# Per-row expert weights: fetched from a table in DRAM instead of spread by products

## What is computed

```python
scores = jax.nn.sigmoid((t @ p['w_router']).astype(jnp.float32))
...
_, e_idx = lax.top_k(jnp.where(e_mask, biased, -jnp.inf), TOP_K)       # TOP_K = 6 of 64
w = jnp.take_along_axis(scores, e_idx, axis=-1)
w = w / jnp.sum(w, axis=-1, keepdims=True) * ROUTE_SCALE
combine = jnp.einsum('tk,tke->te', w, jax.nn.one_hot(e_idx, N_EXPERTS, dtype=jnp.float32)).astype(h.dtype)
gte = jnp.einsum('td,edf->tef', t, p['w_gate_e'])
upe = jnp.einsum('td,edf->tef', t, p['w_up_e'])
routed = jnp.einsum('tef,efd->td', jax.nn.silu(gte) * upe * combine[:, :, None], p['w_down_e'])
```

## Time and profile before

| | |
|---|---|
| median of 3 runs | 992.41 us (990.46 to 992.43) |
| the profiled execution | 994.2 us |
| its span, first to last instruction | 992.6 us |
| mean granted TensorE clock | 0.978 |
| TensorE busy | 923.7 us (93%), weight loads beside it 568.5 (57%) |
| VectorE / ScalarE / GpSimd busy | 339.0 (34%) / 198.4 (20%) / 120.1 (12%) |
| DMA over the span | 324.37 MB, mean 327 GB/s, 57799 packets |

### The profile page before, as it was taken

How to read it: one execution, slowest core, us unless ns; L and a number is a source line. 1 busy time by engine, 2 the same in 40 slices (tenths; PEclk the granted TensorE clock), 3 DMA queues, 4 the chain that set the end, 5 groups by cost and what they waited for, 6 DMA issues and landing times.

```text
span 992.6 us, 18757 instructions
## 1 busy us (share of the span) xinstructions
PE 923.7 (93%) x7759; PEld 568.5 (57%) x7759; DVE 339.0 (34%) x850; ACT 198.4 (20%) x492; POOL 120.1 (12%) x150
## 2 busy tenths in 40 slices
PE   4799999997999689589899999999999999999997
PEld 3688888875565467435755445444444544544542
DVE  0433760046344688616332322221122122222214
ACT  2000110325222277015111111111011111111112
POOL 0000000041573000000110110111011011111100
PEclk9999999999999799889999999999999999999999
DMA  9785666453797736796799999999999999999961
GB/s 374 306 316 237 241 275 234 190 158 134 247 357 261 300 124 236 272 423 268 283 361 413 421 424 421 420 424 422 395 409 425 422 419 422 422 421 423 420 285 67
DMA packets 57799, 324.37 MB, mean 327 GB/s; under 512 B 15089, under 2 KB 25186, under 8 KB 36530
## 3 DMA queue, kind: packets, MB, share of 16 engines
q1 hardware_dynamic: 44930, 304.50, 76.2%
q0 software_dynamic: 11056, 18.47, 5.4%
q10 hardware_dynamic: 1728, 0.18, 0.1%
HBM read 325.59 MB, written 15.74 MB: 344 GB/s over the span
## 4 chain that ended last, share of the span: by engine, by line
PE 49%; DVE 1%; ACT 0%; issue 0%
PE bank L2215 24%; PE bank L2140 12%; PE bank L2151 7%; PE bank L2124 4%; PE bank L2255 1%; PE bank L2161 1%; PE bank L2203 1%; DVE slot_b L2545 0%; DVE slot_b L2553 0%; ACT xt L2337 0%; PE bank L2180 0%; PE bank L2188 0%; ACT slot_b L2363 0%; DVE inv L2552 0%; DVE hh L2444 0%
## 5 line engine op out<-in xcount | busy, mean ns | idle before, releaser
L367 PE MATMUL bank<-h,ring 128*128 128x264 f32 x672 | 154.6, 391 | 2.4 <-DVE h L243 1.8
L367 PEld LDWEIGHTS bank<-h,ring 128*128 128x128 f32 x672 | 127.8, 192 | 26.6 <-issue 3.0
L2346 ACT ACTIVATE sge<-bank 64x256 f32<-64x256 f32 x64 | 24.1, 377 | 409.4 <-PE bank L2215 409.4
L2444 DVE TENSOR_TENSOR hh<-sge,bank 64x256 f32<-64x256 f32 x64 | 27.1, 423 | 227.3 <-ACT sge L2346 227.3
L2215 PE MATMUL bank<-done_out,xt 128*64 128x256 f32 x832 | 95.6, 382 | 0.0
L2215 PE MATMUL bank<-ring,xt 128*64 128x256 f32 x800 | 94.9, 391 | 0.8 <-ACT xt L2337 0.8
L2140 PE MATMUL bank<-ring,ht 128*32 128x512 f32 x336 | 80.2, 598 | 0.0
L2389 DVE COPY sq<-bank 128x512 f32<-128x512 f32 x64 | 44.3, 692 | 102.8 <-PE bank L2140 102.8
L1554 POOL DMA_INDIRECT xg<-tok_rows,tab_g x32 | 32.1, 1002 | 361.4 <-PE bank L2124 349.7
L2215 PEld LDWEIGHTS bank<-done_out,xt 128*64 128x64 f32 x832 | 58.6, 139 | 27.1
L2215 PEld LDWEIGHTS bank<-ring,xt 128*64 128x64 f32 x800 | 57.8, 142 | 28.5 <-issue 3.3
(11 more groups left out here) (476 smaller groups left out, 1197.7 us busy)
## 6 DMA issues: line engine op xcount, KB each, us to landing
ring<-in_w_units SPq DMA_DIRECT2D x28, 2048.0 KB, 10.6
done_out<-in_w_e SPq DMA_DIRECT2D x26, 2048.0 KB, 19.9
ring<-in_w_e SPq DMA_DIRECT2D x25, 2048.0 KB, 19.8
slot_b<-in_w_e SPq DMA_DIRECT2D x13, 2048.0 KB, 20.7
ring<-in_w_e SPq DMA_DIRECT2D x21, 1024.0 KB, 20.9
slot_b<-in_w_e SPq DMA_DIRECT2D x11, 1024.0 KB, 23.2
done_out<-in_w_e SPq DMA_DIRECT2D x11, 1024.0 KB, 19.3
row_of<-in_w_e SPq DMA_DIRECT2D x11, 1024.0 KB, 22.3
```

What stands on the lines that cost most here:

```text
L367: mm = pe.matmul(bank[:, t % NB, 0:T], w[:, j, k, :], h[:, k, :], start=(k == 0), stop=(k == KD - 1))
L2346: act.activation(sg[e % 2][:, :], bank[0:LB, 4, 0:FE], ACT.Silu).then_inc(sg_ready, 1)
L2444: dve.tensor_tensor(hh[e % 2][:, :], sg[e % 2][:, :], bank[LB:2 * LB, 4, 0:FE], ALU.mult).then_inc(hh_ready, 1)
```

## The change

The products that spread the weights are gone. VectorE works out, at the start of the stage, a table of places `tab_w` (row number times 64, plus the expert), in SBUF that another list has left; SP writes `wgt` to a DRAM table `weight_tab` of 264 x 64 numbers in three stores, once `wgt` is ready; and GpSimd issues for each pair one more indirect transfer, which fetches for each of the 128 slots one number of 4 bytes into a column of `wv`. `weight_matrix` takes its weights from that column. The fetch for pair 0 waits for the table. The product for the last samples is replaced by the same column, behind the loop.

```diff
@@ SP, in the loop over experts
                             if e + SLOTS < NE:
                                 load_gu(sp, e + SLOTS)
+                            if e == 0:
+                                sp.wait_ge(wgt_ready, 1)
+                                for a, n, lo in ((0, P, 0), (2, P, P), (1, TS, TP)):
+                                    sp.dma_start(weight_tab[lo * NE:(lo + n) * NE, :].rearrange("(t e) o -> t (e o)", e=NE),
+                                                 wgt[0:n, a, :]).then_inc(tab_stored, 16)
@@ GpSimd
+                        def gather_weights(q):
+                            if q == 0:
+                                pool.wait_ge(tab_stored, 48)
+                            if q >= 2:
+                                pool.wait_ge(w_ready, q - 1)
+                            pool.indirect_dma_start(wv[:, q:q + 1], None, weight_tab,
+                                                    bass.IndirectOffsetOnAxis(ap=tab_w[:, q:q + 1].bitcast(U32), axis=0),
+                                                    bounds_check=T * NE - 1, oob_is_err=False).then_inc(wv_in[q % 2], 16)
                         for q in range(NPAIR):
                             if q + AHEAD < NPAIR:
                                 gather(pool, q + AHEAD)
+                            gather_weights(q)
                             if q >= 2:
                                 scatter_samples(q - 2)
@@ TensorE
-                        def weight_rows(q):
-                            if q == 0:
-                                pe.wait_ge(wgt_ready, 1)
-                            for l in range(2):
-                                for e in (2 * q, 2 * q + 1):
-                                    lo = l * LB + e % 2 * HB
-                                    mm = pe.matmul(bank[lo:lo + HB, 7, P:2 * P], wgt[:, 2 * l, e:e + 1].to_broadcast([P, HB]), ident,
-                                                   start=True, stop=True)
-                            mm.then_inc(wrow_done, 1)
...
-                            if e >= 2:
-                                pe.wait_ge(w_ready, e // 2)
...
-                            if e == LAST_AT:
-                                last_weights()
-                            elif e == LAST_AT + 1:
-                                pe.wait_ge(last_ready, 1)
-                            if e % 2:
-                                weight_rows(e // 2)
@@ VectorE, weights()
+                            place_f = wmat[0][:, 0:NPAIR]
+                            dve.memset(wv, 0.0)
+                            link(dve.tensor_scalar(place_f, tok_f[:, :], float(NE), ccol("second"), ALU.mult, ALU.add))
+                            link(dve.scalar_tensor_tensor(tab_w[:, :], ccol("count")[:, 0:NPAIR], 2.0, place_f, ALU.mult, ALU.add))
@@ VectorE, weight_matrix(q)
-                            dve.wait_ge(wrow_done, q + 1)
+                            dve.wait_ge(wv_in[q % 2], 16 * (q // 2 + 1))
...
-                            dve.scalar_tensor_tensor(wmat[q % 2][:, :], iota, tok_f[:, q:q + 1], bank[:, 7, P:2 * P],
-                                                     ALU.is_equal, ALU.mult).then_inc(w_ready, 1)
+                            dve.tensor_scalar(wmat[q % 2][:, :], iota, tok_f[:, q:q + 1], wv[:, q:q + 1],
+                                              ALU.is_equal, ALU.mult).then_inc(w_ready, 1)
@@ VectorE, in the loop and behind it
-                            elif e == LAST_AT:
-                                dve.wait_ge(last_done, 1)
-                                dve.scalar_tensor_tensor(w_last[:, 0:TS], samples, tok_f[0:LB, NPAIR - 1:NPAIR], bank[0:LB, 7, 256:256 + TS],
-                                                         ALU.is_equal, ALU.mult).then_inc(last_ready, 1)
...
+                        dve.tensor_scalar(w_last[:, 0:TS], samples, tok_f[0:LB, NPAIR - 1:NPAIR], wv[0:LB, NPAIR - 1:NPAIR],
+                                          ALU.is_equal, ALU.mult).then_inc(last_ready, 1)
```

More of the change, by code:

```diff
@@ L112 @@
                   ("valid", NT), ("later", NBLK - NE),
-                  ("count", MAXOVER), ("same_head", NH), ("code", NT), ("side", 4), ("pair", NE // 2)):
+                  ("count", MAXOVER), ("same_head", NH), ("code", NT), ("side", 4), ("pair", NE // 2), ("second", 1)):
     CONSTS[_name] = (_at, _at + _n)
@@ L122 @@
 SHARED_S_AT = 40
-LAST_AT = 50
 def build(nc, io):
@@ L1504, in build @@
         tok_rows = nc.dram_tensor("tok_rows", [T, D], F32, kind="Internal").ap()
+        weight_tab = nc.dram_tensor("weight_tab", [T * NE, 1], F32, kind="Internal").ap()
         choice_rows = nc.dram_tensor("choice_rows", [T * TOPK, D], F32, kind="Internal").ap()
@@ L1994, in build @@
                 tok2 = slot_b[:, 5 * (NBLK - NE):6 * (NBLK - NE)]
+                tab_w, wv = tok_i, tok_j[:, :].bitcast(F32)
                 more_f = slot_b[:, 6 * (NBLK - NE):6 * (NBLK - NE) + (ROUNDS - 1) * HB].rearrange("p (r b) -> p r b", b=HB)
@@ L2008, in build @@
                 ht_done, ht_ready, y_ready = sem("ht_done", ph), sem("ht_ready", ph), sem("y_ready", ph)
-                comb_done, wgt_ready, wrow_done, w_ready = (sem("comb_done", ph), sem("wgt_ready", ph), sem("wrow_done", ph),
-                                                            sem("w_ready", ph))
+                comb_done, wgt_ready, w_ready = sem("comb_done", ph), sem("wgt_ready", ph), sem("w_ready", ph)
+                wv_in = [sem(f"wv_in{i}", ph) for i in range(2)]
                 cnt_done, over_ready, w6_ready, spread_done, wc_ready = (sem("cnt_done", ph), sem("over_ready", ph), sem("w6_ready", ph),
@@ L2023, in build @@
                 scattered, read_back = sem("scattered", ph), sem("read_back", ph)
-                shs_done, shs_took, last_done, last_ready = sem("shs_done", ph), sem("shs_took", ph), sem("last_done", ph), sem("last_ready", ph)
+                shs_done, shs_took, tab_stored, last_ready = sem("shs_done", ph), sem("shs_took", ph), sem("tab_stored", ph), sem("last_ready", ph)
                 half_scaled, rest_ready = sem("half_scaled", ph), sem("rest_ready", ph)
@@ L2190, in shared_rows @@
                             mm.then_inc(shs_done, 1)
[L2192 to L2197, removed]
                         def shared_down(n):
@@ L2666, in constants @@
     put("side", 2 * (r[:, None] // NE) + r[:, None] % 2 == np.arange(4)[None, :])
+    put("second", r[:, None] // HB % 2 - 2)
     put("pair", r[:, None] % NE // 2 == np.arange(NE // 2)[None, :])
```

## The result

The changed kernel takes 997.43 us (median of 9 runs, 994.55 to 997.61), the kernel before beside it 994.11 us (9 runs, 990.46 to 995.41). The ratio is 1.0031, with a 95% interval of 1.0017 to 1.0046: slower by 0.3%, about 3.3 us. The spans of the two profiled executions say 995.7 against 992.6, 3.1 us. Forecast were 8.0 us. The direction was right and the size more than double of what was measured.

A forecast was written before the change was run, and what follows sets the result against it. The prediction took the weight transfers as the floor: 8.0 us later from the start plus 2.9 for packets, less the 2.4 us lead and 0.5 saved behind expert 63, made 8.0 us slower, 1000.4 us; range 990 to 1010.

The forecast's parts named there:

- What bounds the kernel: Expert stage: TensorE sets the end today, but the weight transfers are already slower and TensorE lives on a shrinking lead.
- The need of 15.93 us a pair: Weight queue: time per pair of experts, read from growing landings, where TensorE needed 15.06 us.
- The lead of 2.4 us: At expert 63: weights land at about 967.8, TensorE starts on them at 970.21; limits the gain before that expert.
- TensorE's saving: Removed products: 0.51 us a pair, 16.3 us up to expert 63, and 0.5 us behind it.
- the floor: Expert stage: the transfers' pace limits the end, so a faster TensorE gains only the lead and what it saves behind expert 63.
- The start: Table and first fetch before expert 2: TensorE stands 8.3 us, 11.3 with slow clock; transfers fall 8.0 us behind.
- the slow clock: TensorE at expert 3, after the standstill: its products take 3.0 us more.
- The packets: Fetches in the DMA queue: 144 packets a pair, 0.10 us a pair, 2.9 us before expert 63.
- A: Rival, chance 0.12: TensorE remains the bound over the expert stage and the kernel gets faster, 986.9 us.
- B: Rival, chance 0.09: same floor, but a short standstill costing 2.2 us and free packets; 991.7 us.
- C: Rival, chance 0.05: fetches late for VectorE in every pair; at 10 us late 56 us more, 1056 us.
- The uneven engines: Row gathers: the same few DMA engines carry all filled rows, so a pair needs 15.93 us where even spread gives 15.4.

The follow-up runs named there:

- e2: Changed kernel with only the first half of the down weights loaded from the sixth expert on; 983.22 us against 993.49 before, ratio 0.9909.
- e4: Changed kernel with ranks 8 to 15 of each expert's gathered rows moved to slots 16 to 23; 988.00 us against 991.79 before, ratio 0.9960.
- e9: Changed kernel with each fetch of weights issued three times; 998.36 us against 991.79 before, ratio 1.0094.
- e10: The changed kernel as it is, run again on another chip; 998.29 us against 991.62 before, ratio 1.0053.
- the third experiment: Changed kernel with pairs 0 and 1 by the old products, 988.68 us, ratio 0.9972 to before; with pair 0 alone, 989.93 us, ratio 0.9992.
- the fourth: Changed kernel with each fetch issued three times, 998.36 us, ratio 1.0094 to before; old products kept with unused fetches beside them, 990.80 us, ratio 0.9987.
- e1: Kernel before without the weight-spreading products and without fetches, one constant weight for every row; 986.83 us against 991.79, ratio 0.9961.
- the first two experiments: Kernel before without the products or any fetch, ratio 0.9961 to before; changed kernel with half the down weights loaded from the sixth expert on, 0.9909.
- the edit: Ranks 8 to 15 of an expert moved to slots 16 to 23 of the gather; on the kernel before 992.02 us against 993.49, ratio 0.9995.

## Why the prediction was right in direction and wrong in size

**What bounds the kernel.** Right, and it carried the rest: a busy share of 1.00 on both sides said nothing, and the landings that grew from 16.9 to 28.2 us said that the queue was the slower one. The need of 15.93 us a pair read from them is 15.90 to 16.02 where TensorE waits for it. The lead of 2.4 us was right within the table's accuracy: removing all the products brought 4 us, 2.9 expected. (Two of the thirteen pairs between the two loads are longer, by an extra wait and by other work, and not one; the sum doesn't change.)

**TensorE's saving.** 0.51 us a pair holds for plain pairs; the sum was 1.3 us too high from expert 5 on. It has no part in the result, since the floor hides it.

**The start: the term that was mis-sized.** Its steps were all there: the table, the fetch, VectorE's order, `hh` of expert 2, the slow clock, the dry queue. The sizes: the table landed at 505.99, not 508.7 (about 1.1 us of it because this execution issued the stores sooner, at 501.12 and not at 502.2; the rest because the last store landed 4.0 us after its issue, and not 2 us behind the 2 MB load: by that load's 7.8 us from 497.86 on, it was 0.3 us behind). The fetch took 5.7 us, not 9.5 (5.5 to 6.2 in the traces of e2, e4, e9 and e10): I had priced it by gathers of 4 KB rows, 8.7 to 10.6 us, and even took the smallest of these for the lower bound. I had called this time "mostly waiting its turn beside the weights", and that was wrong: the DMA engines were 93 to 100% busy beside this fetch too. The later fetches do take 10.1 us (median), but they stand right behind a row gather in GpSimd's own queue and land just behind it; the first one had none ahead of it. So TensorE stood 3.7 us at `hh`, not 8.3. The slow clock was right: 2.6 us for 3.0. The transfers fell 4.5 us behind (4 to 6 by all the pairs), not 8.0. This is the step that failed; by the same two traces, 3.5 of the 5 us too many are here.

**The packets.** 2.9 us forecast, 1.1 by the third experiment and 1.3 by the fourth, 1 to 2 us with the comparison against e1. The count was wrong: 128 descriptors and 16 semaphore writes were taken for 144 packets a pair, 9 an engine, and the queue shows 32, two an engine if they are spread evenly. With the forecast's 11 ns that would be 0.6 us; the 1.1 us come to about 20 ns a packet (1.1 us / 29 pairs / 2). So the count was too high and the price of one too low. Why 128 descriptors show as so few packets, no run tells.

**The sum in its place.** 4.5 + 1.1 - 2.4 - 0.5 = 2.7 us, against 3.1 by the spans and 3.3 by the medians. This is a division and no check: start and fetches are both read from the changed kernel's own 481.1 us, so the sum must come out near the spans. What stands on its own is the idle time of the windows for the start, and the fourth experiment for the fetches. The measured 997.4 lies in the range of 990 to 1010, but under half of the forecast change.

**The rivals.** A (TensorE remains the bound) is refuted by the first two experiments. B was the nearest: its mechanism is the forecast's, with 2.2 us for the start and free packets; the truth lies between B and the forecast. C is refuted by VectorE's single wait.

**The uneven engines.** Right in the effect, wrong in a detail: I let the filled rows stand at the start of each block of 32 partitions, which holds for the lists of results. For the gather they stand in partitions 0 to about 48. The Trainium skill (DMA: Bandwidth & Descriptors, The descriptor swizzle) gives half of the engines the lower 64 partitions; by that rule ranks 0 to 7 load these eight engines with four rows each and ranks 8 to 11 load four of them with four more, and the edit moves the latter to the other eight. The end of the queue agrees: a share of 0.50 at 956 to 960 before and then a long tail down to 0.20, with the edit 0.38 there and 0.04 behind. No row names an engine, so the assignment itself isn't shown.

## What to carry to other kernels

Where compute and transfers both look full, read the landings: if the time from issue to landing grows through a stage, the transfers are the slower side, and what a faster engine can gain is only the lead that is left at the stage's end. A new chain at the start of such a stage is paid by the time that the weight queue runs dry, not by the standstill of the engine; it is cheap to keep the old way for the first pair. And try the filled rows of a gather spread over the partitions: here the same bytes were then through 9 us sooner.

## What the runs showed of the hardware that I had not expected

- A fetch of 128 numbers of 4 bytes took 5.7 us with nothing ahead of it in GpSimd's queue, beside DMA engines 93 to 100% busy, and 7.4 to 11.5 us (median 10.1) behind a row gather, about as long as a gather of rows of 4 KB (9.8 to 12.7). The one issued at 750.37 landed 0.7 us behind the gather ahead of it.
- Such a fetch appears as 32 packets in its queue (2048 more for 64 fetches), and costs the queue's pace 1 to 2 us in 30 pairs.
- A standstill of 3.7 us brought TensorE's granted clock to 0.55 to 0.59; 32 records took 6.31 us in place of 3.68.
- The order of slots in a gather was worth 7.5 to 9.3 us over the stage at the same bytes, and 0.5 us a pair (3%) where the queue sets the pace.
